# Gate projections of the mixers as three products of rounded parts, each gate's weights split in place

## What is computed

```python
def hybrid_mixer(h, ...):
    (aq, ak, av, bq, ..., diq, dik, diw) = split(h @ w_in)       # 1024 x 4428
    ya = diff_attention(...)            # unit "a": 4 heads, two softmaxes each
    yb = forgetting_attention(...)      # unit "b": 4 heads
    yc = stick_breaking_attention(...)  # unit "c": 4 heads
    yd = indexed_sparse_attention(...)  # unit "d": 4 heads, after a score and a top-64
    g = sigmoid(h @ w_gate + b_gate)    # 1024 x 4096: the gate projections
    merged = (g[0] * (ya @ w_br_a) + g[1] * (yb @ w_br_b)
              + g[2] * (yc @ w_br_c) + g[3] * (yd @ w_br_d))
    return merged @ w_out
```

## Time and profile before

| | |
|---|---|
| median of three runs | 2840.8 us (2838.07 to 2843.96) |
| the profiled execution | 2842.47 us, its span 2840.7 us, 1.8 us around it |
| PE busy | 2597.0 us, 91% of the span |
| weight loads of PE (overlap it) | 2192.5 us, 77% |
| DVE, ACT, POOL busy | 1443.8, 1191.2, 297.9 us |
| mean granted TensorE clock | 0.945 of full speed |
| gate stretch of layer 0 (first logits to end of gate 31) | 348.7 to 506.4 us |
| the same of layer 1 | 1111.2 to 1268.9 us |

### The profile page before, as it was taken

One profiled execution on the slowest core, in us unless ns is written; L12 is line 12 of the kernel. 1 busy time (PEld: TensorE's weight loads), 2 busy tenths in 40 slices (PEclk: granted clock), 3 DMA queues, 4 the chain that ended last, 5 costly groups with the idle time before them and its releaser, 6 DMA issues.

```text
span 2840.7 us, 52525 instructions
## 1 busy us (share of the span) xinstructions
PE 2597.0 (91%) x23247; PEld 2192.5 (77%) x23247; DVE 1443.8 (51%) x2241; ACT 1191.2 (42%) x1709; POOL 297.9 (10%) x421
## 2 busy tenths in 40 slices
PE   7999899799999999997999999777979889979998
PEld 7997778699999977777998254665457777858886
DVE  5644542656466454436663335332434452158886
ACT  5434374444354345643542034221145432157773
POOL 0100000301001000003110000540123222000000
PEclk9999999899999999998999989887979899989999
DMA  7543423345545443224555631000200002439994
GB/s 239 194 171 128 151 90 119 134 149 178 186 156 171 171 150 127 98 104 148 167 182 183 240 120 60 32 3 14 80 31 4 4 4 94 133 117 366 367 367 146
DMA packets 268885, 396.09 MB, mean 139 GB/s; under 512 B 9320, under 2 KB 172829, under 8 KB 268525
## 3 DMA queue, kind: packets, MB, share of 16 engines
q1 hardware_dynamic: 266921, 389.25, 40.1%
q0 software_dynamic: 1120, 2.17, 0.3%
q10 hardware_dynamic: 612, 1.24, 0.1%
HBM read 391.59 MB, written 1.05 MB: 138 GB/s over the span
## 4 chain that ended last, share of the span: by engine, by line
PE 40%; DVE 7%; issue 5%; DMA 4%; ACT 3%; POOL 2%; SPq 0%; DVEq 0%; POOLq 0%; ACTq 0%
PE ps L271 39%; DMA RB<-in_moe_w_up 4%; DVE gwl L414 2%; ACT gwh L405 1%; POOL H L1249 1%; PE ps L485 1%; POOL AR L1900 0%; POOL AR L2273 0%; DVE AR L1694 0%; DVE AR L1448 0%; DVE AR L1510 0%; DVE AR L1981 0%; POOL AR L1444 0%; ACT L2479 0%; DVE mbwl L414 0%
## 5 line engine op out<-in xcount | busy, mean ns | idle before, releaser
L271 PE MATMUL ps<-H,RB 128*128 128x256 f32 (+1 forms) x1712 | 449.8, 420 | 9.1 <-issue 9.1
L271 PEld LDWEIGHTS ps<-H,RB 128*128 128x128 f32 x1712 | 324.4, 192 | 118.6 <-issue 81.6
L414 DVE TENSOR_TENSOR wl<-RB,wh 128x2048 fp32r<-128x2048 f32 (+1 forms) x136 | 302.8, 2229 | 215.0 <-ACT wh L405 214.5
L271 PE MATMUL ps<-xh,wl 128*128 128x256 f32 x1408 | 400.0, 284 | 0.0
L271 PE MATMUL ps<-xh,wh 128*128 128x256 f32 x1408 | 399.1, 283 | 0.0
L271 PE MATMUL ps<-xl,wh 128*128 128x256 f32 x1408 | 399.1, 283 | 0.0
L271 PE MATMUL ps<-AR 64*64 64x64 f32 (+3 forms) x8296 | 313.7, 245 | 55.8 <-issue 18.0
L271 PEld LDWEIGHTS ps<-AR 64*64 64x64 f32 (+1 forms) x8296 | 263.0, 149 | 111.1 <-issue 81.8
L405 ACT ACTIVATE wh<-RB 128x2048 fp32r<-128x2048 f32 (+1 forms) x136 | 251.6, 1853 | 161.3 <-PE ps L271 122.9
L271 PEld LDWEIGHTS ps<-xl,wh 128*128 128x128 f32 x1408 | 271.1, 193 | 0.1
L271 PEld LDWEIGHTS ps<-xh,wl 128*128 128x128 f32 x1408 | 271.0, 192 | 0.1
(11 more groups left out here) (403 smaller groups left out, 4548.4 us busy)
## 6 DMA issues: line engine op xcount, KB each, us to landing
RB<-in_ffn_w_gu SPq DMA_DIRECT2D x88, 1024.0 KB, 7.7
RB<-in_w_in SPq DMA_DIRECT2D x25, 2048.0 KB, 7.7
RB<-in_ffn_w_down SPq DMA_DIRECT2D x16, 2048.0 KB, 7.8
RB<-in_w_gate SPq DMA_DIRECT2D x16, 2048.0 KB, 8.9
RB<-in_moe_w_gate SPq DMA_DIRECT2D x32, 1024.0 KB, 7.7
RB<-in_moe_w_up SPq DMA_DIRECT2D x32, 1024.0 KB, 10.2
RB<-in_moe_w_down SPq DMA_DIRECT2D x32, 1024.0 KB, 8.1
RB<-in_ada_w SPq DMA_DIRECT2D x12, 2048.0 KB, 7.8
```

Of the source, the lines that this page charges most:

```text
L271: return M.matmul(o, lhsT, rhs, start=start, stop=stop, skip_group_check=True)
L414: V.tensor_tensor(lo, of(slot_of(*key)), hi.bitcast(F32), ALU.subtract).then_inc(*did("low", self.name, h))
```

## The change

The gates now use products of rounded parts too. A new class `GateWeights` splits one gate's 128 x 1024 weights at a time: `high` lets ACT write the rounded copy into one of three buffers (two in `GW`, one in `GX`, which lies where `SG` will hold gates 28 to 31 and is used up to gate 23; from gate 24 on there are two), and `low` lets DVE write the difference **over the weights in their ring slot** (`RBR` is the ring seen as fp32r). Gates 0 and 1 are split at the end of `project`, gate 2 ahead of the list. At the place of gate h in the list, ACT, after the sigmoid of gate h, rounds gate h + 3 (which needs the buffer of gate h, or of gate h + 1 once there are two), and DVE subtracts gate h + 3. The input h is split as well: ACT writes the rounded tiles into the second half of `H` at the end of `project` (`u_high`), and DVE writes the rest over `HA` at the beginning of `attend` (`u_low`). PE's gate is `mm3` on eight tiles, 24 matmuls. `SM` shrinks by four words, and `STAGE` moves down by eight to make room.

```diff
--- before.py
+++ after.py
@@ -72,12 +72,12 @@
...
-    rows="k_rows v_rows rv_rows o_rows u_rows back ob b_rows k_rows_r", h_high="d_high", h_silu="d_silu",
+    rows="k_rows v_rows rv_rows o_rows u_rows back ob b_rows k_rows_r", h_high="d_high gw_high u_high", h_silu="d_silu",
-    copied_v="x_in ctx_v out_v vec", h_low="d_low", h_scaled="c_scaled d_scaled", part_low="m_low y_low", taps="moved",
+    copied_v="x_in ctx_v out_v vec", h_low="d_low", h_scaled="c_scaled d_scaled gw_low u_low", part_low="m_low y_low", taps="moved",
...
@@ -150,7 +150,7 @@
 O_CST, O_RB, O_XT, O_H, O_VEC, O_SM = 0, 3912, 16200, 18248, 22344, 22728
-STAGE = 24032
+STAGE = 24024
@@ -226,8 +226,11 @@
         H = sb("H", O_H, [2, KD * T])
+        RBR = sb("RBR", O_RB, [NSLOT, 4096], F32R)
+        HR = sb("HR", O_H, [2, KD, T], F32R)
         VEC = sb("VEC", O_VEC, [3, 128])
-        SM = sb("SM", O_SM, [1300])
+        SM = sb("SM", O_SM, [1296])
         HA = H[:, 0, :].rearrange("p (k n) -> p k n", k=KD)
@@ -721,11 +724,46 @@
             VN, YT = view(kept, 8192, 2, 1280), view(kept, 10752, 10, T)
-            project(l, PQK, VN, view(kept, 10752, 1024))
-            attend(l, PQK, SG, VN, YT)
+            gw = GateWeights(l, [sb(f"GW{l}", STAGE + 27136, [2, 1024], F32R)[:, i] for i in range(2)]
+                             + [sb(f"GX{l}", STAGE + 7168, [1024], F32R)])
+            project(l, PQK, VN, view(kept, 10752, 1024), gw)
+            attend(l, PQK, SG, VN, YT, gw)
             branches(l, SG, YT)
-        def project(l, PQK, VN, TMP):
+        class GateWeights:
+            def __init__(self, l, bufs):
+                self.l, self.bufs, self.n = l, bufs, [0, 0]
+                self.of = [h % 3 if h < 24 else h % 2 for h in range(32)]
+                self.last = [max((x for x in range(h) if self.of[x] == self.of[h]), default=None) for h in range(32)]
+            def parts(self, h):
+                i, j = divmod(h, 4)
+                slot = job_no["gate", self.l, i] % NSLOT
+                w, lo = (x[:, slot, :].rearrange("p (k n) -> p k n", k=KD)[:, :, 128 * j:128 * j + 128] for x in (RB, RBR))
+                return self.bufs[self.of[h]].rearrange("p (k n) -> p k n", k=KD), w, lo
+            def high(self, upto_gate):
+                while self.n[0] < min(upto_gate, 32):
+                    h = self.n[0]
+                    hi, w, _ = self.parts(h)
+                    AC.wait_ge(*landed("gate", self.l, h // 4))
+                    if self.last[h] is not None:
+                        AC.wait_ge(*at("gate", self.l, self.last[h]))
+                    S.activation(hi, w, ACT.Copy).then_inc(*did("gw_high", self.l, h))
+                    self.n[0] += 1
+            def low(self, upto_gate):
+                while self.n[1] < min(upto_gate, 32):
+                    h = self.n[1]
+                    hi, w, lo = self.parts(h)
+                    DV.wait_ge(*at("gw_high", self.l, h))
+                    V.tensor_tensor(lo, w, hi.bitcast(F32), ALU.subtract).then_inc(*did("gw_low", self.l, h))
+                    self.n[1] += 1
+        def project(l, PQK, VN, TMP, gw):
             st, g = f"p{l}", R_MX + 8 * l
@@ -778,12 +816,17 @@
                     ws.high(2 * gi + 3)
+                    if gi == len(GROUPS) - 1:
+                        gw.high(2)
                     AC.wait_ge(*at("proj", l, gi, 1))
                     AC.wait_ge(*at("by_row", l))
                     for s, lo, hi in evictor(gi, 1)[1]:
                         ins = S.activation(out_of(s, lo, hi, 1), ps_of("proj", l, gi, 1, 1)[:, lo - GROUPS[gi][0]:hi - GROUPS[gi][0]],
                                            ACT.Copy, scale=by_row[:, 1:2])
                     ins.then_inc(*did("seg_a", l, gi))
+                for k in range(KD):
+                    AC.wait_ge(*at("normed", l, k))
+                    S.activation(HR[:, 1, k, :], HA[:, k, :], ACT.Copy).then_inc(*did("u_high", l, k))
@@ -795,6 +838,8 @@
                     ws.low(2 * gi + 3)
+                    if gi == len(GROUPS) - 1:
+                        gw.low(2)
                     DV.wait_ge(*at("proj", l, gi, 1))
@@ -829,7 +874,7 @@
-        def attend(l, PQK, SG, VN, YT):
+        def attend(l, PQK, SG, VN, YT, gw):
             ar = sb(f"AT{l}", STAGE + 13312, [13824])
@@ -903,12 +948,13 @@
                     if kind == "gate":
-                        i, j = divmod(h, 4)
-                        sv = slot_of("gate", l, i).rearrange("p (k n) -> p k n", k=KD)
-                        PE.wait_ge(*landed("gate", l, i))
+                        hi, _, lo = gw.parts(h)
+                        PE.wait_ge(*at("gw_low", l, h))
                         ps = bank(("gate", l, h), ("gated", l, h))
                         for k in range(KD):
-                            ins = mm(ps[:, 0:T], sv[:, k, 128 * j:128 * j + 128], HA[:, k, :], k == 0, k == KD - 1)
+                            PE.wait_ge(*at("u_low", l, k))
+                            ins = mm3(ps[:, 0:T], (hi[:, k, :], lo[:, k, :]),
+                                      (HR[:, 1, k, :], HR[:, 0, k, :]), k == 0, k == KD - 1)
                         ins.then_inc(*did("gate", l, h))
@@ -979,11 +1025,13 @@
                 AC.wait_ge(*at("iw", l))
+                gw.high(3)
                 for kind, h, phase in order:
                     if kind == "gate":
                         AC.wait_ge(*at("gate", l, h))
                         S.activation(SG[:, h, :], ps_of("gate", l, h)[:, 0:T], ACT.Sigmoid,
                                      bias=vec(R_BG + 32 * l + h)).then_inc(*did("gated", l, h))
+                        gw.high(h + 4)
                     elif kind == "score" and phase < 8:
@@ -1024,6 +1072,10 @@
             def vector():
+                for k in range(KD):
+                    DV.wait_ge(*at("u_high", l, k))
+                    V.tensor_tensor(HR[:, 0, k, :], HA[:, k, :], HR[:, 1, k, :].bitcast(F32), ALU.subtract).then_inc(
+                        *did("u_low", l, k))
                 for i in range(2):
@@ -1045,8 +1097,11 @@
                 DV.wait_ge(*at("cq", l))
+                gw.low(3)
                 for kind, h, phase in order:
-                    if kind == "score":
+                    if kind == "gate":
+                        gw.low(h + 4)
+                    elif kind == "score":
                         score(phase)
```

## The result

The changed kernel takes **2880.7 us** (median; 2877.4 to 2885.0) against 2839.4 (2836.9 to 2844.0) of the kernel before on the same chip: a ratio of 1.0145, 95% interval 1.0125 to 1.0164, 41 us more. The profiled execution took 2877.4 us (span 2875.7).

What follows compares the result with a forecast made beforehand. PE bounds the attention stage. Per layer: -18 gain, +2 start, +33.6 waits, -1.1 today's waits, +6 clock = +22; two layers +44 us, from 2842.5 to 2886.5 profiled, 2885 as median; range 2850 to 2925.

Steps and rivals of the forecast that it cites:

- The gain: Gates of two layers as three rounded products: 0.56 us saved a gate, 18 a layer, 36 in all.
- four passes: Skill's account of true fp32 on PE: three products would take 2.6 us a gate, gain 52 us; not adopted.
- The start: Subtracting h on DVE ahead of the attention stage delays the first logits: +2 us a layer.
- The waits: PE's waits a layer: 13 us in rounds 0 to 7, 8 in 8 to 17, 12.6 in 18 to 21: 33.6.
- circle: DVE waits for ACT's rounding, ACT for PE's gate, PE for DVE's queued work: 8.3 us in round 2 or 3.
- The clock: Half clock after PE waits of 3.4 us or longer, four a layer: 0 to 13 us a layer, taken as 6.
- The sum: Gain, start, waits less today's 1.1, and clock: +22 us a layer, +44 in two layers, 2885 us.
- Look-ahead suffices: Rival: three gates of look-ahead hide the new work, only the start is left: -32 us, 2809; chance 0.12.
- About even: Rival: half of PE's forecast waits and no clock loss: 0 us, 2841; chance 0.06.
- The clock stays low: Rival: PE waits of 2 to 3 us drop the clock too: 2905 or 2917, up to 2940; chance 0.16.
- The return to half rate: Skill's rule: idle gaps between bursts put PE's array back to half rate every loop turn; time near 2940.

Runs made afterwards that it cites:

- e1: The change without splitting gates 2 to 31, PE multiplying by the rounded copy of gate 0 or 1: 2813.3 us, ratio 0.9915 to the kernel before.
- e8: e7 with the eight subtractions of the hidden state on DVE behind its copies of turned queries and keys: 2828.8 us, ratio 0.9969.
- e9: The change with DVE subtracting only 8 of each 128 columns from gate 3, rounded weights used as both parts: 2852.3 us, ratio 1.0041.
- e10: e9 with ACT's rounding also cut to 8 of each 128 columns: 2831.9 us, ratio 0.9959.
- e11: e8 with, up to gate 21, ACT rounding at the round's score entry and DVE subtracting only what is already rounded ahead: 2826.1 us, ratio 0.9954.
- e7: The change with subtraction a gate later, three buffers to gate 27, roots and first reciprocal earlier, second behind gate 31's subtraction: 2833.9 us, ratio 0.9985.
- e5: The change with dummy PE products ahead of its waits of over 2 us: 2867.4 us, ratio 1.0106.
- e12: e11 with dummy PE products before c3, a0 and d3 (10, 8 and 38): 2828.1 us, ratio 0.9974.
- e4: The change with the subtraction of the gates' weights on POOL instead of DVE: 2867.0 us, ratio 1.0102.

## Why the prediction was right, point by point

- **The gain.** Predicted 18 us a layer (0.56 us a gate). In PE's timeline of the change, gates 5 and 6, the first of each three products:

```profile
386.90 0.28 PE L274 MATMUL ps<-HR,RBR 128*128 128x256 f32 x1
...
391.49 0.28 PE L274 MATMUL ps<-HR,RBR 128*128 128x256 f32 x1
```

  Thirteen threes in 4.59 us are 0.353 each, 0.118 a product, 2.83 a gate. The 3.51 of before hold a hand-over beside the records, so the like of it is the 5.86 us that these two gates take from their first product to the next one behind them, 2.93 a gate: 0.58 us a gate, 19 a layer. PE's busy time less the lost part fell by 19 to 20 us a layer in the change (22 in e1, where gates 2 to 31 need no splitting and come one behind the other more closely). So this term was right within 2 us in the change. By the four passes of the Trainium skill (FP8 and Floating Point Precision, TensorE Precision Notes) the prediction had an estimate of 2.6 us a gate; that would be a gain of 58 us, not the 52 that it wrote. Neither is borne out: the rows give 0.58 x 64 = 37, by busy time 39.
- **The start.** Predicted +2; +1.8 in layer 0 and +2.6 in layer 1, and the eight subtractions, which e8 moves away, are most of it.
- **The waits.** The step as the prediction put it was 13 + 8 + 12.6 = 33.6 us a layer; measured 9.2 + 6.0 + 9.6 = 24.7. The places were right: a2 2.9 (3.6 predicted), b0 1.3 (2.1), b3 1.8 (2.4), d0 2.4 (3.0), gate 29 3.1 (3.4), gate 31 4.1 (5.5), each measured 10 to 40% below its forecast. Only the longest of the early rounds was misplaced: c1, behind two gates in one round (2.6), not c3 in round 6 (1.8). That DVE's and ACT's new work does it by its place in the circle is shown by e9, e10 and e11 together, and N2's part, along with that of the buffers, by e7.
- **The clock.** Predicted 6 us a layer within bounds of 0 and 13; lost 15.7 and 11.8, so this term was mis-sized, in layer 0 beyond its upper bound. The prediction let only waits of over 3 us count, as in the kernel before, and here waits of 2.4 to 2.9 were followed by the half clock too. Not all of it was on the path: e5 took 19 of the 27 us away and got 11 back, up to 3.7 of the rest being the dummies' own. In that proportion some 8 us a layer or more were on the path, above the 6 of the sum.
- **The sum.** +22 a layer predicted; +21 and +18 measured. Waits over-sized by 9 a layer and lost clock under-sized by 10 and 6 cancelled each other for the most part. That the total is better than its terms is luck; the mechanism, a circle whose waits eat the gain, is not.
- **The rivals.** Look-ahead suffices: out, for TensorE waits 25 us a layer. About even: out, for the ratio's interval begins at 1.0125. The clock stays low: it fell six times a layer and came back each time after 3 to 10 us. The return to half rate of which the Trainium skill (TensorE: Matmul & The Clock Gate, HAM oscillation) tells is there, in 34 us of layer 0's stretch and 24 of layer 1's, not in every round.

## What to carry to other kernels

Before moving work from the bound engine to two idle ones, do not ask whether they have time in sum, but where each new piece stands in their order: here two engines with a third and more of their time idle turned a gain of 24 us into a loss of 41, and moving lines (subtract a gate later, root earlier, second reciprocal later, split the input behind the copies, round behind the logarithms), with one buffer kept longer and the same work, brought 54 back. Put new work that a later step needs behind the work that the next step needs, and let no engine stop for it in front of something urgent. And filling an idle gap for the clock's sake gives something back only if the dummies are done before the operand is there: 19 us less lost gave 11 in e5, and in e12 dummies at a place without a wait ate up the 1.0 us won at another.

## What was not expected of the hardware

- **The length of a single wait does not decide the clock.** In the change waits of 2.61 us (before 374.30) and 2.42 (before 499.83) were followed by the half clock; in e11 one of 2.56 at nearly the same place (372 to 374.8) was not, and two shorter ones (1.34 and 1.53, with little between) were:

```profile
374.00:376.00 2.00, 1.20 (x8) 1.05 (x10) 1.79 (x4) 1.98 (x4) 0.00 (x0) 1.00 0.00 0
376.00:378.00 2.00, 2.00 (x19) 1.85 (x19) 1.63 (x3) 1.97 (x3) 0.00 (x0) 1.00 0.04 12
...
388.00:390.00 2.00, 0.69 (x4) 0.67 (x5) 1.29 (x4) 1.99 (x5) 0.00 (x0) 1.00 0.45 87
...
392.00:394.00 2.00, 0.54 (x4) 0.57 (x5) 1.97 (x10) 1.96 (x4) 0.00 (x0) 1.00 1.05 409
394.00:396.00 2.00, 2.00 (x12) 2.00 (x11) 0.45 (x4) 2.00 (x8) 0.00 (x0) 0.53 0.51 189
```

  What rule lies behind that stays open.
- **An operation of two elements can cost 2.3 us.** In e4 POOL's subtraction of 128 x 1024 took 2.39 us beside DVE's 1.22 for the same, and DVE's 128 x 2 operations of lines 1140, 1142 and 1144 that met one were held to its end (1.6 to 2.3 us instead of 0.16 or 0.17), while its maxima (0.42 us), its copies out of PSUM (0.43) and its top-8 operations (0.41) were not. So it is not a slower DVE but a stop, and only for some forms of operation. Which property of the form decides was not tested.
- The unchanged part after layer 1 differed by 4.6 us between the two profiled executions, which is nearly what a measurement can tell.
